# Routing table of an expert layer: the token ids summed from bfloat16 one-hots before the weights, and the first gather issued from the id table inside the routing's block

## The chip, the core and the metric

One core of a Trainium2 chip runs the whole kernel in one launch. Its engines run side by side and meet by semaphores: PE (TensorE) multiplies matrices into PSUM, DVE (VectorE) and ACT (ScalarE) work on elements, POOL (GpSimd) makes constants and issues the indirect DMAs, SP (SyncE) issues the plain ones. The metric is the device time of one execution in microseconds (us): the median of three runs before was 1134.75 (1132.99 to 1135.12).

## The reference, cut to what matters

One decoder layer: 1024 prompt tokens and 64 sample tokens (8 by 8) of width 1024 pass a mixer (attention and convolution), a residual add, a norm, and then 16 experts of which each token uses two.

```
h = rmsnorm(y + mix @ w_out)                       # 1088 rows
g_idx = argmax(h @ w_group + b_group)              # one of 4 groups; g_w its softmax weight
e_val, e_idx = top_k((h @ w_router + b_router)[group g_idx], 2)
e_w = softmax(e_val) * g_w
combine[n, e] = e_w of the two chosen experts, else 0
hid = silu(h @ w_gate[e]) * (h @ w_up[e]) * combine
y = y + sum over e of hid @ w_down[e];  out = rmsnorm(y)
```

## The kernel before, in words

The kernel is a row of blocks: projection, attention, `mix_out` (output projection, residual, norm, routing) and `experts`. A block holds a program for each engine; between two blocks all engines meet in a barrier, which POOL collects and releases. The order inside an engine is as written; nothing is scheduled.

`mix_out` goes over nine tiles of 128 tokens (the last has 64): it stores x1 and the normed h as rows in memory and makes the router's logits. After the last tile comes the routing, most of it a chain on DVE. Each token has two chosen experts (k = 0, 1). The pairs are sorted by expert into blocks of 128 slots, at most MAXB = 32 blocks; `slot_f` is a pair's slot, `block_f` its block and `row_f` its row there. Two tables are wanted, with 128 rows and one column for each block: `slot_ids` (the token of a slot) and `slot_w` (its weight). They come from one-hots: `block_pick` (which block, 32 columns, L1716) is multiplied by the weights (L1718) and by the token numbers plus one (L1720), `row_pick` (which row, 128 columns, L1724, three tiles at a time) turns it, and PE sums `row_pick`^T x `block_pick` over nine tiles, two choices and two halves of the rows: 72 matmuls in float32 (L1834). An empty slot sums to 0 and is given a spare row's number (L1735, L1736). `slot_w` is copied last (L1738). Meanwhile ACT rounds the first expert's up weights (`up_hi`, L1883); each float32 weight tile is kept as a rounded part, `_hi` on ACT, and the remainder, `_rest` on DVE (L1888), and PE multiplies with both.

`experts` goes over the blocks. For each one POOL copies a column of `slot_ids` to `row_id` (L2026) and issues an indirect DMA that gathers 128 rows of h into `landing` (L2029). DVE copies `landing` to `rows` (`fetch`, L2140), PE turns `rows` by transposes (L2212), ACT rounds (`rowsT_hi`) and DVE takes the remainder (`rowsT_lo`, L2145). PE makes gate and up, DVE the product `hid`, PE turns it, ACT and DVE split it (`hidT_hi`, `hidT_lo`), and PE makes y, which ACT and DVE scale by `slot_w` into `y_out`; POOL adds that to x1 in memory. Gathers run ahead: `gather(b)` waits until block b-1's rows were copied out of `landing`. Before the first block DVE makes `up_rest`, then fetches. SP loads the second expert's weights (gate, up, down; 2 MB each) when the first gather has landed, and every later expert's when PE has done with the buffer:

```
sp.wait_ge(gathered, 16)
for which in moe.names:
    moe.load(sp, which, 1, 1)
```

DVE in the first step makes `down_rest` and a half of the next `gate_rest` before `hid`; ACT makes `gate_hi` (a half), silu, `gate_hi` and `up_hi` (a half each) before `hidT_hi`.

Of the kernel before, what the change touches and what calls it, by code (L numbers as in the profile page):

```python
# [24 lines left out]
BF16 = mybir.dt.bfloat16  # L25
# [4 lines left out]
P = 128  # L30
# [1351 lines left out]
def mix_out(nc, io, keep):  # L1382
# [5 lines left out]
    PAIRS = NB // 2  # L1388
    with ExitStack() as stack:  # L1389
# [50 lines left out]
        token_no = p.sb("token_no", [P, TT])  # L1440
# [4 lines left out]

        row_pick = keep["stage"][:, D * KD // 2:D * KD // 2 + 2 * TT * P].rearrange("p (t k x) -> p t k x", t=TT, k=2)
        block_pick = keep["stage"][:, D * KD // 2 + 2 * TT * P:D * KD // 2 + 2 * TT * (P + 2 * MAXB)].rearrange("p (t k v x) -> p t k v x", t=TT, k=2, v=2)
# [77 lines left out]
        def _(pool):  # L1525
# [5 lines left out]
            nc.gpsimd.iota(token_no[:, :], pattern=[[P, TT]], base=1, channel_multiplier=1, **exact).then_inc(consts, 1)  # L1531
            pool.wait_ge(consts, 3)
            nc.gpsimd.memset(token_no[NB * NT:P, QT_N:TT], 0.0).then_inc(consts, 1)
# [15 lines left out]
                                    pattern=[[1, NE], [-1, NE]], channel_multiplier=0).then_inc(consts, 1)  # L1549

        @block.scalar
        def _(act):
# [34 lines left out]
            nc.scalar.activation(e_exp[:, :], e_gap[:, :], ACT.Exp).then_inc(e_exped, 1)  # L1587
            for c in range(2):
                moe.split_hi(act, "up", 0, 0, c)

        @block.vector
        def _(dve):
# [59 lines left out]
            for t in range(TT):  # L1652
# [29 lines left out]
                if t in SELECT_AFTER:  # L1682
# [31 lines left out]

            all_slots = [P, TT, 2, MAXB]
            step(nc.vector.tensor_tensor(block_pick[:, :, :, 0, :], iota_p[:, 0:MAXB].unsqueeze(1).unsqueeze(1).to_broadcast(all_slots),  # L1716
                                         block_f[:, :, :].unsqueeze(3).to_broadcast(all_slots), ALU.is_equal))
            step(nc.vector.tensor_tensor(block_pick[:, :, :, 1, :], block_pick[:, :, :, 0, :],  # L1718
                                         weight[:, :, :].unsqueeze(3).to_broadcast(all_slots), ALU.mult))
            step(nc.vector.tensor_tensor(block_pick[:, :, :, 0, :], block_pick[:, :, :, 0, :],  # L1720
                                         token_no[:, :].unsqueeze(2).unsqueeze(2).to_broadcast(all_slots), ALU.mult))
            for t in range(0, TT, 3):
                part = [P, 3, 2, P]
                nc.vector.tensor_tensor(row_pick[:, t:t + 3, :, :], iota_p[:, :].unsqueeze(1).unsqueeze(1).to_broadcast(part),  # L1724
                                        row_f[:, t:t + 3, :].unsqueeze(3).to_broadcast(part), ALU.is_equal).then_inc(slotted, 1)
            step(nc.vector.memset(ends_f[:, 0:1], 0.0))
# [4 lines left out]
            step(nc.vector.memset(slot_ids[:, MAXB:], 0))  # L1731
            dve.wait_ge(slots_summed, 1)
            numbers = y[0][0][:, 0:MAXB]

            step(nc.vector.tensor_scalar(occupied[:, :], numbers, 0.0, spare_no[:, 0:1], ALU.is_equal, ALU.mult))  # L1735
            step(nc.vector.scalar_tensor_tensor(out=slot_ids[:, 0:MAXB], in0=occupied[:, :], scalar=-1.0, in1=numbers,  # L1736
                                                op0=ALU.add, op1=ALU.add))
            step(nc.vector.tensor_copy(slot_w[:, 1:], y[0][0][:, MAXB:2 * MAXB]))  # L1738

        @block.tensor  # L1740
        def _(pe):
# [150 lines left out]
def experts(nc, io, keep):  # L1892
# [5 lines left out]
    with ExitStack() as stack:  # L1898
# [489 lines left out]
```

## Time and profile before

| | |
|---|---|
| median of three runs | 1134.75 us |
| the profiled execution, its span | 1136.06 us, 1134.3 us |
| PE busy | 1040.3 us (92%) |
| DVE, ACT, POOL busy | 595.7 (53%), 482.1 (43%), 152.5 (13%) us |
| mean granted clock of PE | 0.965 |
| moved by DMA | 207.31 MB, 183 GB/s |

Busy shares are means over stages with different limits. A row of the timeline has the start in us from the span's start, the length in us, the engine, the line of the kernel, the operation, out<-in by names, shapes and the count of merged instructions; in brackets the engine's idle time before and what ended it. `stage` is the buffer that holds `row_pick` and `block_pick`, so their rows carry its name. PEclk is the granted share of PE's full clock: 0.50 is 1.2 GHz, 1.00 is 2.4 GHz.

### The profile page before, as it was taken

What the parts mean: (1) busy time and instruction counts of PE and PEld (TensorE: products, weight loads), DVE (VectorE), ACT (ScalarE), POOL (GpSimd) and SP (SyncE); (2) the same over time, 40 slices, a digit from 0 to 9 for tenths busy, and PEclk for the clock granted to TensorE, in tenths of its full rate; (3) what the DMA queues carried; (4) which work ended last, traced back from release to release, by engine and by line L of the source; (5) the groups of instructions that cost most, each with busy time, mean ns of one, the idle gap of its engine ahead of it and who ended that gap; (6) DMA issues with size and microseconds to landing.
All of it is one profiled execution on the core that took longest, in us unless ns stands there. A gap on an engine that the chain in (4) does not pass through costs nothing. (4 is left out here: it accounts for less than half of the span.)

```text
span 1134.3 us, 16350 instructions
## 1 busy us (share of the span) xinstructions
PE 1040.3 (92%) x5907; PEld 853.1 (75%) x5908; DVE 595.7 (53%) x976; ACT 482.1 (43%) x748; POOL 152.5 (13%) x139
## 2 busy tenths in 40 slices
PE   4999999999899998989999469999999999999990
PEld 3779999999766656648888358888888778888870
DVE  4421351110266664534255755566599967458845
ACT  5431110111466663433333253355468745537544
POOL 0000000000100000000000032122235341323320
PEclk8999999999999999999999679999999999999995
DMA  6416121012540006656332576668799976869766
GB/s 215 130 47 257 56 57 56 13 45 78 137 140 1 1 1 224 264 225 218 125 125 104 184 277 211 184 209 286 252 381 378 370 252 253 296 207 366 245 196 242
DMA packets 95873, 207.31 MB, mean 183 GB/s; under 512 B 12560, under 2 KB 34873, under 8 KB 95787
## 3 DMA queue, kind: packets, MB, share of 16 engines
q1 hardware_dynamic: 88332, 179.89, 44.3%
q0 software_dynamic: 7488, 26.71, 8.8%
q8 instruction: 33, 0.54, 0.2%
q14 instruction: 20, 0.16, 0.0%
HBM read 175.75 MB, written 37.08 MB: 188 GB/s over the span
## 5 line engine op out<-in xcount | busy, mean ns | idle before, releaser
L605 PE MATMUL bank<-xT_hi,w_hi 128*128 128x384 f32 (+1 forms) x432 | 94.6, 327 | 0.0
L605 PE MATMUL bank<-xT_rest,w_hi 128*128 128x384 f32 (+1 forms) x432 | 93.9, 325 | 0.0
L605 PE MATMUL bank<-xT_hi,w_rest 128*128 128x384 f32 (+1 forms) x432 | 93.9, 325 | 0.0
L2048 POOL DMA_INDIRECT x_rows<-y_out,out_id x23 | 57.8, 2512 | 170.5 <-DVE rows L2140 156.4
L2255 PE MATMUL y<-down_hi,hidT_hi 128*128 128x512 f32 x192 | 77.0, 401 | 2.2 <-ACT hidT_hi L2102 2.2
L2220 PE MATMUL gate<-gate_hi,rowsT_hi 128*128 128x512 f32 x192 | 76.7, 399 | 0.7 <-ACT rowsT_hi L2077 0.7
L1888 DVE TENSOR_TENSOR down_rest<-w_down,down_hi 128x2048 fp32r<-128x2048 f32 x32 | 71.9, 2288 | 10.3 <-ACT down_hi L1883 9.4
L2221 PE MATMUL gate<-gate_rest,rowsT_hi 128*128 128x512 f32 x192 | 77.2, 402 | 0.0
L2221 PE MATMUL up<-up_rest,rowsT_hi 128*128 128x512 f32 x192 | 75.7, 394 | 0.0
L1888 DVE TENSOR_TENSOR gate_rest<-w_gate,gate_hi 128x2048 fp32r<-128x2048 f32 x32 | 73.1, 2284 | 4.7 <-ACT gate_hi L1883 4.7
L2220 PE MATMUL up<-up_hi,rowsT_hi 128*128 128x512 f32 x192 | 75.2, 392 | 0.0
L2256 PE MATMUL y<-down_rest,hidT_hi 128*128 128x512 f32 x192 | 75.1, 391 | 0.0
L605 PEld LDWEIGHTS bank<-xT_hi,w_rest 128*128 128x128 f32 x432 | 73.0, 188 | 0.0
L605 PEld LDWEIGHTS bank<-xT_hi,w_hi 128*128 128x128 f32 x432 | 72.7, 188 | 0.2
L605 PEld LDWEIGHTS bank<-xT_rest,w_hi 128*128 128x128 f32 x432 | 72.3, 188 | 0.0
L1888 DVE TENSOR_TENSOR up_rest<-w_up,up_hi 128x2048 fp32r<-128x2048 f32 x32 | 71.8, 2285 | 0.6 <-PEq L1389 0.6
L1883 ACT ACTIVATE up_hi<-w_up 128x2048 fp32r<-128x2048 f32 x32 | 61.5, 1924 | 10.0 <-DMA w_up<-in_w_up 9.9
L1883 ACT ACTIVATE gate_hi<-w_gate 128x2048 fp32r<-128x2048 f32 x32 | 61.3, 1914 | 5.5 <-DMA w_gate<-in_w_gate 5.4
L1883 ACT ACTIVATE down_hi<-w_down 128x2048 fp32r<-128x2048 f32 x32 | 59.7, 1916 | 0.8 <-issue 0.7
L2166 DVE TENSOR_TENSOR hid<-up,silu 128x128 f32<-128x128 f32 (+1 forms) x48 | 18.1, 420 | 71.0 <-PE up L2224 71.0
L998 ACT ACTIVATE logit<-logit,neg_max 128x256 f32<-128x256 f32 (+7 forms) x80 | 52.2, 656 | 6.3 <-DVE neg_max L1082 6.3
L2026 POOL COPY row_id<-slot_ids 128x1 int32 (+1 forms) x26 | 34.3, 1321 | 149.0 <-POOLq L1389 137.3
(310 smaller groups left out, 2083.1 us busy)
## 6 DMA issues: line engine op xcount, KB each, us to landing
w_gate<-in_w_gate SPq DMA_DIRECT2D x16, 2048.0 KB, 12.9
w_up<-in_w_up SPq DMA_DIRECT2D x16, 2048.0 KB, 13.6
w_down<-in_w_down SPq DMA_DIRECT2D x16, 2048.0 KB, 15.4
stage<-in_w_in SPq DMA_DIRECT2D x6, 1536.0 KB, 7.0
k_cache<-in_cache_b_k SPq DMA_DIRECT2D x8, 768.0 KB, 6.7
bias_scratch<-bias_one_row SPq DMA_DIRECT2D x1, 5800.0 KB
mixT<-in_x_prompt SPq DMA_DIRECT2D x8, 512.0 KB, 4.1
x<-in_x_prompt SPq DMA_DIRECT2D x8, 512.0 KB, 4.4
```

The lines of the kernel that those rows point to most:

```text
L605: ins = nc.tensor.matmul(bank[3 * (n % 2) + i][:, 0:m], w_tiles(wt, n // CH + 1)[:, k, cols], xt[:, k, c:c + m], start=(k == 0 and x == 0) ...
L998: nc.scalar.activation(logit[:, u % 4, 0:n], logit[:, u % 4, 0:n], ACT.Exp, bias=neg_max[:, u:u + 1], scale=-1.0, accum_out=denom[:, u:u + ...
L1883: self.nc.scalar.activation(self.hi[which][half][:, k, :], self.raw[which][half][:, k, :], ACT.Copy).then_inc(self.hi_made, 1)
L1888: self.nc.vector.tensor_tensor(self.rest[which][half][:, k, :], self.raw[which][half][:, k, :], self.hi[which][half][:, k, :].bitcast(F32) ...
L2026: nc.gpsimd.tensor_copy(row_id[:, :], slot_ids[:, bass.ds(b, 1)]).then_inc(gather_id, 1)
L2048: nc.gpsimd.indirect_dma_start(out=io["x1"], out_offset=bass.IndirectOffsetOnAxis(ap=out_id[:, :], axis=0), in_=y_out[:, :], in_offset=Non ...
L2166: nc.vector.tensor_tensor(hid[:, cols], up[:, cols], silu[:, cols], ALU.mult).then_inc(hid_ready, 1)
L2220: nc.tensor.matmul(out[:, :], rowsT_hi[:, k, :], hi[:, k, :], start=(k == 0), stop=False)
L2221: nc.tensor.matmul(out[:, :], rowsT_hi[:, k, :], rest[:, k, :], start=False, stop=False)
L2255: nc.tensor.matmul(y[j][:, :], hidT_hi[:, k, :], moe.hi["down"][half][:, k, cols], start=(k == 0), stop=False)
L2256: nc.tensor.matmul(y[j][:, :], hidT_hi[:, k, :], moe.rest["down"][half][:, k, cols], start=False, stop=False)
```

## The change

The sum over slots is split in two. The first sum makes the ids alone. `row_pick_b` (bfloat16) takes the place of `row_pick` in it, and the token numbers enter as whole numbers that bfloat16 holds exactly: ACT makes `row_no` = `block_pick` x (row + 1) for all tiles, and `tile_no` = `block_pick` x 128 t for tiles 1 to 8. PE adds both kinds: 34 matmuls over whole 128 rows. Pairs that don't exist get row -1. Then `slot_ids` is written, and only then DVE multiplies `block_pick` by the weights, writes `ends`, and waits for the second sum: 72 float32 matmuls as before with 32 columns in place of 64, for which ACT converts `row_pick_b` to float32 `row_pick`, before `up_hi`.

POOL issues the first gather at the end of `mix_out`, with a column of `slot_ids` as its index and without a copy, into `first_rows`, a part of `mixT` (free by then). In `experts` the second gather waits for no fetch; DVE fetches first and makes `up_rest` after `rowsT_lo`; SP waits for `rows_ready`, since `first_rows` lies where the second expert's weights go.

On DVE, from the rows of the slots to the second fetch, before (the stage's names stand for `block_pick` and `row_pick`):

```order
L1712 SCALAR_TENSOR_TENSOR row_f<-block_f,slot_f 128x18 [waits dve_step3]
L1716 TENSOR_TENSOR stage<-iota_p,block_f 128x18x32 [waits dve_step3]
L1718 TENSOR_TENSOR stage<-stage,weight 128x18x32 [waits dve_step3]
L1720 TENSOR_TENSOR stage<-stage,token_no 128x18x32 [waits dve_step3]
L1724 TENSOR_TENSOR stage<-iota_p,row_f 128x768 [waits dve_step3]
...
L1735 TENSOR_SCALAR occupied<-y,spare_no 128x32 [waits slots_summed,dve_step3]
L1736 SCALAR_TENSOR_TENSOR slot_ids<-occupied,y 128x32 [waits dve_step3]
L1738 COPY slot_w<-y 128x32 [waits dve_step3]
...
L1888 TENSOR_TENSOR up_rest<-w_up,up_hi 128x2048 [waits weights_hi] x2
L2140 COPY rows<-landing 128x1024 [waits gathered]
L2145 TENSOR_TENSOR rowsT_lo<-turn,rowsT_hi 128x512 [waits rowsT_hi_made] x2
```

and of the changed kernel:

```order
L1733 SCALAR_TENSOR_TENSOR row_f<-block_f,slot_f 128x18 [waits dve_step3]
L1737 MEMSET row_f 64x2 [waits dve_step3]
L1739 TENSOR_TENSOR stage<-iota_p,block_f 128x576 [waits dve_step3]
L1743 TENSOR_TENSOR row_pick_b<-iota_p,row_f 128x768 x3
L1748 TENSOR_SCALAR occupied<-y,spare_no 128x32 [waits slots_summed]
L1749 SCALAR_TENSOR_TENSOR slot_ids<-occupied,y 128x32 [waits dve_step3]
L1753 TENSOR_TENSOR stage<-stage,weight 128x576 [waits gapped,e_exped]
...
L1762 COPY slot_w<-y 128x32 [waits slots_summed,dve_step3]
...
L2170 COPY rows<-mixT 128x1024 [waits gathered]
L2175 TENSOR_TENSOR rowsT_lo<-turn,rowsT_hi 128x512 [waits rowsT_hi_made] x2
L1919 TENSOR_TENSOR up_rest<-w_up,up_hi 128x2048 [waits weights_hi] x2
L2170 COPY rows<-landing 128x1024 [waits gathered,turned5]
```

The product with the weights went behind the ids, the one with the token numbers left DVE, and `up_rest` went behind the first fetch. On POOL, from the routing's last constant to the second gather, before:

```order
L1548 AFFINE_SELECT ahead<-ahead_blocks 128x256 [waits consts3]
L1389 UNCONDITIONAL_BRANCH
L2020 UNCONDITIONAL_BRANCH [waits barrier_Pool_Activation_PE_DVE_SP_gather]
L2026 COPY row_id<-slot_ids 128x1
L2029 DMA landing<-h_rows,row_id 128x1024 [waits gather_id]
L2026 COPY row_id<-slot_ids 128x1 [waits rows_ready]
L2029 DMA landing<-h_rows,row_id 128x1024 [waits gather_id]
```

and of the changed kernel:

```order
L1552 AFFINE_SELECT ahead<-ahead_blocks 128x256 [waits consts3]
L1561 DMA mixT<-h_rows,slot_ids 128x1024 [waits spare_stored,slotted,h_stored1,mix_rest_made,h_stored0]
L1390 UNCONDITIONAL_BRANCH
L2051 UNCONDITIONAL_BRANCH [waits barrier_Pool_Activation_PE_DVE_SP_gather]
L2057 COPY row_id<-slot_ids 128x1
L2060 DMA landing<-h_rows,row_id 128x1024 [waits gather_id]
```

The first gather stands ahead of the barrier, and its copy is gone. On ACT, between the last exponential and the end of the block, the changed kernel has (before, the two `up_hi` followed at once):

```order
L1600 ACTIVATE e_exp<-e_gap 128x9 [waits gapped]
L1603 ACTIVATE row_no<-stage,row_one 128x576 [waits consts3,gapped]
L1605 ACTIVATE tile_no<-stage 128x64 x8
L1608 ACTIVATE stage<-row_pick_b 128x768 [waits slotted] x3
L1914 ACTIVATE up_hi<-w_up 128x2048 [waits up_loaded0]
L1914 ACTIVATE up_hi<-w_up 128x2048
```

Twelve instructions came in ahead of `up_hi`. The diff, cut to its core:

```diff
...
@@ mix_out, POOL
-            nc.gpsimd.iota(token_no[:, :], pattern=[[P, TT]], base=1, channel_multiplier=1, **exact).then_inc(consts, 1)
+            nc.gpsimd.iota(row_one[:, :], pattern=[[0, 1]], base=1, channel_multiplier=1, **exact).then_inc(consts, 1)
...
+            pool.wait_ge(mix_rest_made, TT)
+            pool.wait_ge(h_stored[0], 16 * 5)
+            pool.wait_ge(h_stored[1], 16 * 4)
+            pool.wait_ge(spare_stored, 32)
+            pool.wait_ge(slotted, TT // 3 + 1)
+            nc.gpsimd.sem_inc(consts, 1)
+            nc.gpsimd.indirect_dma_start(out=first_rows, out_offset=None, in_=io["h"],
+                                         in_offset=bass.IndirectOffsetOnAxis(ap=slot_ids[:, 0:1], axis=0)).then_inc(gathered, 16)
@@ mix_out, ACT, behind e_exp
+            act.wait_ge(gapped, 2)
+            act.wait_ge(consts, 4)
+            nc.scalar.activation(row_no[:, :, :, :], block_pick[:, :, :, :], ACT.Copy, scale=row_one[:, :]).then_inc(e_exped, 1)
+            for t in range(1, TT):
+                nc.scalar.activation(tile_no[:, t - 1, :, :], block_pick[:, t, :, :], ACT.Copy, scale=float(P * t)).then_inc(e_exped, 1)
+            for j in range(TT // 3):
+                act.wait_ge(slotted, j + 1)
+                nc.scalar.activation(row_pick[:, 3 * j:3 * j + 3, :, :], row_pick_b[:, 3 * j:3 * j + 3, :, :], ACT.Copy).then_inc(e_exped, 1)
             for c in range(2):
                 moe.split_hi(act, "up", 0, 0, c)
...
@@ mix_out, PE
             for t in range(TT):
-                if t % 3 == 0:
-                    pe.wait_ge(slotted, t // 3 + 1)
+                pe.wait_ge(slotted, t // 3 + 1)
+                pe.wait_ge(e_exped, 2 + t)
+                for k in range(2):
+                    nc.tensor.matmul(y[0][0][:, 0:MAXB], row_pick_b[:, t, k, :], row_no[:, t, k, :], start=(t == 0 and k == 0), stop=False)
+                    if t:
+                        ins = nc.tensor.matmul(y[0][0][:, 0:MAXB], row_pick_b[:, t, k, :], tile_no[:, t - 1, k, :], start=False, stop=(t == TT - 1 and k == 1))
+            ins.then_inc(slots_summed, 1)
+            pe.wait_ge(slotted, TT // 3 + 2)
+            pe.wait_ge(e_exped, 1 + TT + TT // 3)
+            for t in range(TT):
                 for k in range(2):
                     for rows in (slice(0, P // 2), slice(P // 2, P)):
-                        ins = nc.tensor.matmul(y[0][0][rows, 0:2 * MAXB], row_pick[:, t, k, rows],
-                                               block_pick[:, t, k, :, :].rearrange("p v x -> p (v x)"),
+                        ins = nc.tensor.matmul(y[0][1][rows, 0:MAXB], row_pick[:, t, k, rows], block_pick[:, t, k, :],
                                                start=(t == 0 and k == 0), stop=(t == TT - 1 and k == 1))
             ins.then_inc(slots_summed, 1)
@@ experts, SP, POOL and DVE
-            sp.wait_ge(gathered, 16)
+            sp.wait_ge(rows_ready, 1)
...
-                if b is not FIRST:
+                if type(b) is not int or b > 1:
                     pool.wait_ge(rows_ready, b)
...
-            gather(FIRST)
             gather(1)
...
-                nc.vector.tensor_copy(rows[:, :], landing[:, :]).then_inc(rows_ready, 1)
+                nc.vector.tensor_copy(rows[:, :], first_rows if b is FIRST else landing[:, :]).then_inc(rows_ready, 1)
...
-            for c in range(2):
-                moe.split_rest(dve, "up", 0, 0, c)
             fetch(FIRST)
             rows_lo(FIRST, 0)
             rows_lo(FIRST, 1)
+            for c in range(2):
+                moe.split_rest(dve, "up", 0, 0, c)
             fetch(1)
...
@@ program
+        keep["first_rows"] = keep["mixT"][:, 0, 0:D]
```

## Rows read from the trace of the kernel before

**Rows 1.** PE, 676 to 1095 us: who it waited for, total us, times, longest.
```profile
PE y L2255 <- ACT hidT_hi L2102: 2.2, 2, 1.2
PE hturn L2245 <- DVE hid L2166: 1.5, 1, 1.5
```

**Rows 2.** Timeline, ACT and DVE at the second expert's weights (columns as above).
```profile
669.36 1.92 ACT L1883 ACTIVATE gate_hi<-w_gate 128x2048 fp32r<-128x2048 f32 x1 [2.23 <-DMA w_gate<-in_w_gate]
...
675.96 1.91 ACT L1883 ACTIVATE up_hi<-w_up 128x2048 fp32r<-128x2048 f32 x1 [0.96 <-DMA w_up<-in_w_up]
...
677.28 0.75 DVE L2166 TENSOR_TENSOR hid<-up,silu 128x128 f32<-128x128 f32 x2
...
677.98 0.28 ACT L2102 ACTIVATE hidT_hi<-hturn 128x128 fp32r<-128x128 f32 x1
```

**Rows 3.** The same timeline, SP's issues of the second expert's weights.
```profile
659.31 0.38 SPq L1874 DMA_DIRECT2D w_gate<-in_w_gate  x1
...
659.74 0.57 SPq L1874 DMA_DIRECT2D w_up<-in_w_up  x1
```

**Rows 4.** The same timeline, DVE at the end of the routing.
```profile
641.68 0.18 DVE L1712 SCALAR_TENSOR_TENSOR row_f<-block_f,slot_f 128x18 f32<-128x18 f32 x1
...
641.89 0.76 DVE L1716 TENSOR_TENSOR stage<-iota_p,block_f 128x576 f32<-128x576 f32 x1
...
644.27 2.69 DVE L1724 TENSOR_TENSOR stage<-iota_p,row_f 128x768 f32<-128x768 f32 x3
...
649.41 0.25 DVE L1735 TENSOR_SCALAR occupied<-y,spare_no 128x32 f32<-128x32 f32 x1 [1.69 <-PE y L1834]
...
649.70 0.19 DVE L1736 SCALAR_TENSOR_TENSOR slot_ids<-occupied,y 128x32 int32<-128x32 f32 x1
...
649.92 0.19 DVE L1738 COPY slot_w<-y 128x32 f32<-128x32 f32 x1
```

**Rows 5.** The same timeline, PE: the count's first pass, the sum over slots.
```profile
636.95 0.39 PE L1824 MATMUL count<-picks,ones 128*128 128x16 bf16 x9 [4.75 <-DVE picks L1688]
...
645.28 4.01 PE L1834 MATMUL y<-stage 128*64 128x64 f32 x72 [7.32 <-DVE stage L1724]
```

**Rows 6.** ACT by shape, 560 to 680 us (busy, mean ns); one timeline row.
```profile
L1557 ACT ACTIVATE mix_hi<-mixT 128x1024 fp32r<-128x1024 f32 x3 | 3.1, 1046 | 0.0
...
L1585 ACT ACTIVATE g_exp<-g_shift 128x36 f32<-128x36 f32 x1 | 0.2, 233 | 1.0 <-DVE g_shift L1630 1.0
...
641.39 3.71 ACT L1883 ACTIVATE up_hi<-w_up 128x2048 fp32r<-128x2048 f32 x2 [5.36 <-DMA w_up<-in_w_up]
```

**Rows 7.** The timeline, POOL: the first two gathers.
```profile
650.72 2.29 POOL L2026 COPY row_id<-slot_ids 128x1 int32<-128x1 int32 x1 [137.32 <-POOLq L1389]
...
653.95 2.23 POOL L2029 DMA_INDIRECT landing<-h_rows,row_id  x1 [0.94 <-POOL row_id L2026]
...
660.08 0.18 POOL L2026 COPY row_id<-slot_ids 128x1 int32<-128x1 int32 x1 [3.90 <-DVE rows L2140]
...
661.06 0.96 POOL L2029 DMA_INDIRECT landing<-h_rows,row_id  x1 [0.80 <-POOL row_id L2026]
```

**Rows 8.** The timeline, DVE at the start of the experts.
```profile
650.67 4.49 DVE L1888 TENSOR_TENSOR up_rest<-w_up,up_hi 128x2048 fp32r<-128x2048 f32 x2 [0.56 <-PEq L1389]
...
659.32 0.69 DVE L2140 COPY rows<-landing 128x1024 f32<-128x1024 f32 x1 [4.16 <-DMA landing<-h_rows,row_id]
...
662.70 0.69 DVE L2145 TENSOR_TENSOR rowsT_lo<-turn,rowsT_hi 128x512 fp32r<-128x512 f32 x1 [0.16 <-ACT rowsT_hi L2077]
...
669.08 0.69 DVE L2140 COPY rows<-landing 128x1024 f32<-128x1024 f32 x1 [5.69 <-DMA landing<-h_rows,row_id]
```

**Rows 9.** Gathers into landing, from issue to landing.
```profile
DMA to landing us min/median/max: 5.1/8.7/10.0
```

**Rows 10.** Two stretches: busy us of each engine, PEclk, DMA share, GB/s.
```profile
653.00:666.00 13.00, 5.25 (x16) 4.17 (x17) 4.24 (x4) 3.78 (x4) 3.38 (x4) 0.50 0.53 175
...
667.00:680.00 13.00, 11.53 (x57) 9.31 (x56) 9.08 (x10) 9.17 (x10) 4.57 (x3) 1.00 1.03 395
```

More of the change, by code:

```diff
@@ L1388, in mix_out @@
     PAIRS = NB // 2
+    gathered, first_rows = keep["gathered"], keep["first_rows"]
     with ExitStack() as stack:
@@ L1439, in mix_out @@
         weight = p.sb("weight", [P, TT, 2])
-        token_no = p.sb("token_no", [P, TT])
+        row_one = p.sb("row_one", [P, 1])
         spare_no = p.sb("spare_no", [P, 1])
@@ L1446, in mix_out @@
         row_pick = keep["stage"][:, D * KD // 2:D * KD // 2 + 2 * TT * P].rearrange("p (t k x) -> p t k x", t=TT, k=2)
-        block_pick = keep["stage"][:, D * KD // 2 + 2 * TT * P:D * KD // 2 + 2 * TT * (P + 2 * MAXB)].rearrange("p (t k v x) -> p t k v x", t=TT, k=2, v=2)
+        block_pick = keep["stage"][:, D * KD // 2 + 2 * TT * P:D * KD // 2 + 2 * TT * (P + MAXB)].rearrange("p (t k x) -> p t k x", t=TT, k=2)
+        row_pick_b, row_no = keep["row_pick_b"], keep["row_no"]
+        tile_no = p.sb("tile_no", [P, TT - 1, 2, MAXB], BF16)
         zeros = p.sb("zeros", [P, 128])
@@ L1713, in _ @@
                                                 op0=ALU.mult, op1=ALU.add))
+            step(nc.vector.memset(row_f[NB * NT:P, QT_N, :], -1.0))
             all_slots = [P, TT, 2, MAXB]
[L1716 to L1721, printed above, removed]
+            nc.vector.tensor_tensor(block_pick[:, :, :, :], iota_p[:, 0:MAXB].unsqueeze(1).unsqueeze(1).to_broadcast(all_slots),
+                                    block_f[:, :, :].unsqueeze(3).to_broadcast(all_slots), ALU.is_equal).then_inc(gapped, 1)
             for t in range(0, TT, 3):
                 part = [P, 3, 2, P]
-                nc.vector.tensor_tensor(row_pick[:, t:t + 3, :, :], iota_p[:, :].unsqueeze(1).unsqueeze(1).to_broadcast(part),
+                nc.vector.tensor_tensor(row_pick_b[:, t:t + 3, :, :], iota_p[:, :].unsqueeze(1).unsqueeze(1).to_broadcast(part),
                                         row_f[:, t:t + 3, :].unsqueeze(3).to_broadcast(part), ALU.is_equal).then_inc(slotted, 1)
+            dve.wait_ge(slots_summed, 1)
+            numbers = y[0][0][:, 0:MAXB]
+            step(nc.vector.tensor_scalar(occupied[:, :], numbers, 0.0, spare_no[:, 0:1], ALU.is_equal, ALU.mult))
+            nc.vector.scalar_tensor_tensor(out=slot_ids[:, 0:MAXB], in0=occupied[:, :], scalar=-1.0, in1=numbers,
+                                           op0=ALU.add, op1=ALU.add).then_inc(slotted, 1)
+            dve.wait_ge(e_exped, 1 + TT)
+            dve.wait_ge(gapped, 2)
+            nc.vector.tensor_tensor(block_pick[:, :, :, :], block_pick[:, :, :, :],
+                                    weight[:, :, :].unsqueeze(3).to_broadcast(all_slots), ALU.mult).then_inc(slotted, 1)
+            step(nc.vector.memset(slot_ids[:, MAXB:], 0))
             step(nc.vector.memset(ends_f[:, 0:1], 0.0))
@@ L1730, in _ @@
             step(nc.vector.tensor_copy(ends[:, :], ends_f[:, :]))
[L1731 to L1738, printed above, removed]
+            dve.wait_ge(slots_summed, 2)
+            step(nc.vector.tensor_copy(slot_w[:, 1:], y[0][1][:, 0:MAXB]))
         @block.tensor
@@ L1920, in experts @@
         rows_ready = p.sem("rows_ready")
-        gathered = p.sem("gathered")
+        gathered, first_rows = keep["gathered"], keep["first_rows"]
         gather_id = p.sem("gather_id")
@@ L2329, in program @@
             keep["silu"] = q.sb("silu", [P, FF])
+        with ExitStack() as later:
+            q = Pools(nc, later)
+            q.sb("first_rows_place", [P, D])
+            keep["row_pick_b"] = q.sb("row_pick_b", [P, TT, 2, P], BF16)
+            keep["row_no"] = q.sb("row_no", [P, TT, 2, MAXB], BF16)
         keep["mixT"] = p.sb("mixT", [P, 8, TOK])
@@ L2351, in program @@
                 attend(nc, io, keep)
+        keep["gathered"] = p.sem("gathered")
+        keep["first_rows"] = keep["mixT"][:, 0, 0:D]
         moe.place(p, 0)
```

4 lines of the change are left out of this document (2 added, 2 removed).

## The prediction

> **What bounds the kernel now.** I began with the page: PE is busy for 92% of the span, and its row of slices shows one clear hole, in the slice where attention's output has been projected and the experts have not begun. The waits of PE from 676 us to the last expert say the same from the other side: in over 400 us it waits 3.7 us in all, and all of that beside the first expert's hidden rows [rows 1]. From there on PE sets the time, and every weight load is released by PE's progress, so whatever the first expert's hidden rows gain reaches the end.
>
> So the timeline around those rows came next [rows 2]. ACT splits three weight tiles of the second expert in a row; the first waited for w_gate and began at 669.36, the last waited for w_up and began at 675.96. It ended at 677.87, and hidT_hi, queued behind it on ACT, began at 677.98, just when PE's turned rows were there. Two chains meet here within 0.1 us: the hidden rows (DVE's hid at 677.28) and the second expert's weights. The weights start when SP issues them, at 659.31, 659.74 and after [rows 3]: w_gate needs 10.05 us, w_up 16.2 us, with the DMA rings at 395 GB/s [rows 10]. SP waits for the first gather. So both chains hang on one thing: when the first block's rows of h have landed.
>
> Then backward from there. DVE's table work ends with row_pick, the three comparisons from 644.27 to 646.96; PE sums 72 pieces until 649.29; slot_ids is written by 649.89, slot_w by 650.11 [rows 4, 5]. The experts' block opens 0.56 us later: up_rest begins at 650.67 [rows 8], and POOL copies the ids (2.29 us) and issues the gather at 653.95 (2.23 us) [rows 7]. The rows land at 659.3, 9.4 us after the ids were written. The second gather's same two steps took 0.18 and 0.96 us. The first ones ran beside up_rest, 650.67 to 655.16; the copy ended at 653.01, with the first half of up_rest (2.29 us a half), and the issue 1.0 us after the second half.
>
> The Trainium skill ("SBUF — State Buffer", Who interferes with whom) states that a DVE instruction with two SBUF inputs blocks a GpSimd instruction that reads SBUF; the copy agrees with that (2.29 against 0.18 us). The same section infers that it doesn't hold back descriptor generation; the issue's 2.23 against 0.96 us speaks against this part. By the page the second gather could not be held by up_rest, which would strike rival 2 below; by the row it could.
>
> **The change, part by part.**
>
> Ids. DVE's two products over block_pick leave the path; they are 576 wide like the comparison at 641.89, which took 0.76. A memset of row_f comes in; I charge it a whole step, the 0.21 from row_f's start to the next. block_pick then runs 642.10 to 642.86, and three row_pick_b comparisons (2.69 together, same width) end at 645.56 instead of 646.96. Their output type changes; I leave the price.
>
> Beside them ACT makes row_no and eight tile_no. ACT's price is read from 1.046 us at 1024 columns and 0.233 at 36 [rows 6], that is 0.20 + 0.82 per 1000 columns: 0.68 for row_no (576), 0.26 for each tile_no (64). Two instructions in a row overlap by 0.1 (3.71 for two up_hi [rows 6], 1.91 for one [rows 2]), so the eight cost 1.2 to 2.1, and ACT is through between 644.8 and 645.7: level with DVE.
>
> PE's id sum is 34 matmuls with bfloat16 weights; the nearest row is the nine of the count, 0.39 us together, 0.043 each [rows 5]. When the last row_pick_b comes, 12 are left: 0.5 us. The other bound is the old pace, 4.01/72 = 0.056, with all 34 after the last comparison: 1.9 us. I take 0.5 and 0.1 for the wait: the sum ends at 646.2 (at worst 647.6). The ids follow 0.60 after, as from 649.29 to 649.89: 646.8, at worst 648.2, instead of 649.89.
>
> First gather. POOL needs no copy; it waited 0.80 to 0.94 before each issue [rows 7], which I keep: issue at 647.7. It takes 0.96 alone or 2.23 beside DVE. The product with the weights, moved behind the ids, runs 646.9 to 647.6 and is over by then. In the profile the rows landed 3.1 us after the issuing ended, so 651.8; the shortest from issue to landing is 5.1 us [rows 9], which gives 652.8, or 654.2 with the late ids. No other transfer runs then.
>
> The block's end. This is now what comes last. ACT converts three row_pick pieces (768 columns, 0.84 each), which begins when its small pieces are done: the last ends between 646.4 and 648.2. Then up_hi, 3.71, until 650.1 to 651.9; before it was done by 645.1, so work that cost nothing now reaches the path. PE's second sum waits for the converted pieces and for the weighted block_pick (647.7); 72 matmuls with the same stationary width and half the columns cost 2.0 to 4.0, so they end between 649.8 and 652.2, and slot_w stands 0.3 later. DVE's five small steps on ends lie under this. Block entry is 0.56 after the last: 651.0 to 653.1; I take 652.6, near the upper end, where the measured 4.01 stands.
>
> First rows. DVE's fetch, now first in the experts' block, starts at the later of entry and landing, 652.6 (bounds 651.5 and 654.2), instead of 659.32; with 0.69 for the copy rows_ready comes at 653.3. SP now waits for rows_ready, not for the landing; so its loads start at 653.3 instead of 659.31: **6.0 us earlier** (4.4 to 7.1). That is the term which counts. The rows themselves come 6.7 earlier (660.01).
>
> What is late next. up_rest lost its cover: it used to lie under the gather's landing and now stands between rows_lo and the second fetch. rows_lo ended 3.38 us after the rows were copied (663.39 after 660.01 [rows 8]), so 656.7; up_rest's 4.49 gives 661.2. The up product begins when gate is through, 7.4 us after gate's start at 656.0 with the clock at half (0.50 until 666 [rows 10]) and earlier at full clock by less than 2 us: up_rest is in time or barely late. The second gather waits no longer for rows_ready. POOL's copy may stand behind DVE's fetch (to 653.5), the issue follows at 654.3 and ends at 655.3; at 7.0 us from there, as with the weights in flight before (662.02 to 669.05), it lands at 662.3, and the second fetch ends at 663.0. From there to hid it was 7.51 us (669.77 to 677.28): 670.5, a gain of 6.8. w_up lands 6.0 earlier, at 669.9; up_hi ends at 671.9 and hidT_hi follows. So the weights' 6.0 stays the smaller gain and PE gets 6.0. A faster PE clock in this stretch gives nothing: PE would wait for the same two.
>
> Sum: the profiled execution took 1136.06 us, 1.8 more than its span of 1134.3 and 1.3 above the median of the runs, 1134.75. 1136.06 - 6.0 = 1130.1 for that execution, and against the median 1134.75 - 6.0 = **1128.75, I say 1128.8 us**.
>
> **The rivals.**
> 1. The block's end holds more than I gave it. For it: ACT gets 12 instructions more on the path, and waits between engines of 0.1 us are hardly in my sum. If the chain of conversions, second sum and slot_w comes 1 to 3 us later (entry 654.3 to 656), the gain is 2.3 to 4.4: 1130.4 to 1132.5. Against it: each price has a near row.
> 2. The second gather is held by up_rest, as the first was. Condition: its issue isn't through at 656.7; I have it through at 655.3, 1.4 us of margin. Behind one half of up_rest it would end at 656.7 + 2.29 + 0.96 = 659.9, land at 666.9, and hid would come at 675.2: 2.1 gained, 1132.7. Behind both, the issue ends at 662.1, hid comes at 677.2: nothing gained, 1134.7.
> 3. Slower: the same holding behind both halves, and a landing of 10.0 us from the issue, the longest in the trace [rows 9], because the weights are then in full flight. Issue at 661.2, landing 671.2, hid 679.4: 2.1 later than now, 1136.9. It decides from the point where landing plus 0.69 plus 7.51 passes 677.28, that is a landing after 669.1. Against it: both must come together.
> 4. More: the weights are not the limit (they land sooner in a freer stretch) and entry is early, at 651.5. Then hid's gain of 6.8 grows to 7.9: 1126.9. Against it: 395 GB/s is steady in the trace.
> 5. The first gather doesn't run ahead, since POOL's queue reaches it late or the block's end waits for its landing. The five semaphores it waits for are all met before the ids, and a landing at 651.8 before the block's end adds at most 0.6: this only joins rival 1.
>
> **How the numbers follow.** Forecast (4.4 to 7.1 gained) 0.60; rival 1 with 5, 0.15; rival 2, 0.11; rival 3, 0.04; rival 4, 0.10. About 0.2% of this kernel, 2.3 us, can be told from no change. Faster: forecast, rivals 1 and 4, less a hundredth, 0.84. Same: rival 2 (2.1 and 0 gained) and that hundredth, less some for noise to either side, 0.11. Slower: rival 3 and a hundredth of rival 2, 0.05. The range holds the forecast, rival 4 nearly whole and two thirds of rival 1: 1126.7 to 1131.7.
>
> **What would show it.** Right: slot_ids written near 646.8; the first DMA_INDIRECT near 647.7 with a length near 1.0; DVE's first fetch at 652.6, ended waiting by the block's opening and not by the landing; SP's w_gate at 653.3; ACT's second up_hi in the experts' block still waiting for w_up, and hidT_hi 6 us earlier; PE's waits after 670 as few as before. Wrong: the fetch waits for the landing after 653; up_hi in the routing block ends after 653; the second DMA_INDIRECT takes over 2 us; or PE waits for up_rest before the first up product.

## The result and the profile after

The changed kernel took 1125.9 us (median of 4 runs, 1123.21 to 1126.21) beside 1134.37 us for the kernel before (4 runs, 1132.99 to 1135.12): the ratio of the times is 0.9917 [0.9902, 0.9932]. That is 8.5 us by the medians, where 6.0 were forecast, and 0.8 us below the range. Two later pairings gave 0.9921 [0.9902, 0.994] and 0.9936 [0.9914, 0.9957].

The timeline of the changed kernel, from DVE's row_f to the third expert's first weight load (start in us, length in us, engine, line, operation, tiles, and in brackets the idle time before it with what ended it):

```profile
639.67 0.18 DVE L1733 SCALAR_TENSOR_TENSOR row_f<-block_f,slot_f 128x18 f32<-128x18 f32 x1
...
640.68 2.69 DVE L1743 TENSOR_TENSOR row_pick_b<-iota_p,row_f 128x768 bf16<-128x768 f32 x3
...
641.48 1.26 ACT L1605 ACTIVATE tile_no<-stage 128x64 bf16<-128x64 f32 x8
...
643.42 0.21 PE L1857 MATMUL y<-row_no,row_pick_b 128*128 128x32 bf16 x1 [0.27 <-DVE row_pick_b L1743]
...
644.25 0.19 DVE L1749 SCALAR_TENSOR_TENSOR slot_ids<-occupied,y 128x32 int32<-128x32 f32 x1
...
644.85 3.69 ACT L1914 ACTIVATE up_hi<-w_up 128x2048 fp32r<-128x2048 f32 x2
...
645.16 4.05 PE L1866 MATMUL y<-stage 128*64 128x32 f32 x72 [1.23 <-DVE stage L1753]
645.50 1.14 POOL L1561 DMA_INDIRECT mixT<-h_rows,slot_ids  x1 [134.38 <-DVE stage L1753]
649.33 0.19 DVE L1762 COPY slot_w<-y 128x32 f32<-128x32 f32 x1 [3.47 <-PE y L1866]
...
650.31 0.69 DVE L2170 COPY rows<-mixT 128x1024 f32<-128x1024 f32 x1 [0.79 <-PEq L1390]
650.37 0.68 POOL L2057 COPY row_id<-slot_ids 128x1 int32<-128x1 int32 x1 [3.73 <-POOLq L1390]
651.03 0.38 SPq L1905 DMA_DIRECT2D w_gate<-in_w_gate  x1
651.46 0.57 SPq L1905 DMA_DIRECT2D w_up<-in_w_up  x1
651.84 0.97 POOL L2060 DMA_INDIRECT landing<-h_rows,row_id  x1 [0.79 <-POOL row_id L2057]
...
659.95 0.69 DVE L2170 COPY rows<-landing 128x1024 f32<-128x1024 f32 x1 [1.17 <-DMA landing<-h_rows,row_id]
...
667.00 1.91 ACT L1914 ACTIVATE up_hi<-w_up 128x2048 fp32r<-128x2048 f32 x1 [0.47 <-DMA w_up<-in_w_up]
668.15 0.75 DVE L2196 TENSOR_TENSOR hid<-up,silu 128x128 f32<-128x128 f32 x2
...
668.86 0.28 ACT L2132 ACTIVATE hidT_hi<-hturn 128x128 fp32r<-128x128 f32 x1
...
680.90 0.41 SPq L1905 DMA_DIRECT2D w_gate<-in_w_gate  x1
```

The row of the kernel before that answers to the last of these is

```profile
690.02 0.41 SPq L1874 DMA_DIRECT2D w_gate<-in_w_gate  x1
```

Read all of them against [rows 4, 7, 8, 2, 3] as well, and count from row_f in both traces. The ids start 4.58 us after row_f instead of 8.02, the gather's issue 5.83 instead of 12.27, DVE's copy of the first rows 10.64 instead of 17.64, SP's first load 11.36 instead of 17.63, DVE's copy of the second rows 20.28 instead of 27.40, hid 28.48 instead of 35.60. The third expert's first load, which PE's progress releases, starts 41.23 after row_f instead of 48.34: 7.1 us gained in this stretch, as much as the copy of the second rows gained. The two profiled spans differ by 10.1. The other 3.0 lie outside: row_f itself stands at 639.67 instead of 641.68 (2.0), and the third load to the end takes 443.3 instead of 444.3 (1.0).

PE's waits from 655 to 1090 us (total us, times, longest) answer to [rows 1]; the pair of chains still meets there, hidT_hi at 668.86 with up_hi from 667.00 just over:

```profile
PE y L2285 <- ACT hidT_hi L2132: 2.1, 2, 1.2
PE hturn L2275 <- DVE hid L2196: 1.0, 1, 1.0
```

Three stretches just before the experts' block opens, and w_up's way from its issue to its split (length, busy us of PE, its weight loads, DVE, ACT and POOL, then PE's granted clock, DMA share and GB/s):

```profile
648.00:649.00 1.00, 1.00 (x24) 1.00 (x22) 0.00 (x0) 0.54 (x1) 0.00 (x0) 0.50 0.92 356
649.00:649.50 0.50, 0.22 (x5) 0.08 (x2) 0.17 (x1) 0.00 (x0) 0.00 (x0) 0.50 0.49 180
649.50:650.00 0.50, 0.00 (x0) 0.00 (x0) 0.02 (x1) 0.00 (x0) 0.00 (x0) 0.50 0.00 0
...
651.46:667.00 15.54, 14.85 (x58) 11.77 (x57) 11.94 (x9) 10.52 (x8) 5.14 (x4) 0.80 0.97 347
```

The last two columns matter: the traffic ends by 649.50, and slot_w, the last of the second sum, is written by 649.52. DVE's copy follows at 650.31, 0.8 us after both, ended waiting by the block's opening. From this trace alone nobody can say which of the two it waited for.

### The profile page after: what moved, and what is told of

Same layout as the page of the kernel before. It is cut to its first block and busy times, and to the rows that moved or that the text cites. A ratio compares the mean times of both kernels' runs of the same rounds, so it can differ in the third digit from the quotient of the medians.

```text
span 1124.2 us, 16421 instructions
## 1 busy us (share of the span) xinstructions
PE 1041.0 (93%) x5941; PEld 854.3 (76%) x5942; DVE 594.3 (53%) x976; ACT 486.3 (43%) x760; POOL 145.5 (13%) x138
## 5 line engine op out<-in xcount | busy, mean ns | idle before, releaser
L2078 POOL DMA_INDIRECT x_rows<-y_out,out_id x23 | 49.2, 2140 | 177.9 <-DVE rows L2170 163.8
L2132 ACT ACTIVATE hidT_hi<-hturn 128x128 fp32r<-128x128 f32 (+1 forms) x48 | 18.2, 383 | 80.0 <-PE hturn L2275 80.0
```

The costliest lines, as they stand in the source:

```text
L2078: nc.gpsimd.indirect_dma_start(out=io["x1"], out_offset=bass.IndirectOffsetOnAxis(ap=out_id[:, :], axis=0), in_=y_out[:, :], in_offset=Non ...
L2132: nc.scalar.activation(hidT_hi[:, k0:k1, :], hturn[c][:, 0:(k1 - k0) * P].rearrange("p (k c) -> p k c", c=P), ACT.Copy).then_inc(hidT_hi_m ...
```

## The experiments

Throughout, "third load" is the third expert's first weight load, counted from row_f; it was 48.34 before and 41.23 in the changed kernel. Where times are compared, the ratio is to the kernel before on the same chip.

**The two kernels again.** No edit; the changed kernel twice more, the kernel before twice more.

> The changed kernel once more, for its time over more rounds and a second profile. In the first pair of profiles the routing's chain stood 2.0 us earlier before any changed instruction (row_f began at 639.67 against 641.68), 7.2 us were gained between row_f and the third expert's first load, and 1.0 us after that. Theory 1: only the 7.2 us come from the change; the rest is stretches of half clock in attention that differ from one execution to the next, so row_f lands anywhere between 639 and 642.5 here, the length from row_f to the third expert's load is again within 0.3 us of 41.2, and over five rounds the gain comes to 7 to 7.6 us (ratio 0.9933 to 0.9938). Theory 2: the new program also runs its unchanged parts faster, by 1 to 2 us: row_f again within 0.3 us of 639.7 and a gain of 8.2 to 9 us (0.9921 to 0.9928).

> The kernel before, timed against itself. Both theories: ratio 1.000 within 0.1%. Theory 1: row_f in its profile moves by up to 2 us from 641.68 while the length from row_f to the third expert's load stays at 48.3 within 0.4 us. Theory 2: row_f stays within 0.3 us of 641.7.

The changed kernel: third load 41.26 and, beside a later experiment, 41.36. The kernel before: 50.44 here (ratio to itself 0.999 [0.9974, 1.0007]) and 47.92 in a further profile. So the changed kernel repeats its stretch within 0.13 us, and the kernel before does not repeat its own within 2.5, where 0.4 was expected. The first expectation is met by half: row_f and the stretch came as its first theory has them, the ratio, 0.9921, as its second; the interval holds both. The mean gain over three profiles each is 48.90 - 41.28 = 7.6. Row_f stands at 641.68, 639.72 and 637.63 before and at 639.67, 640.54 and 639.16 after: no part of the gain is there, so I take the 2.0 between the first two profiles for scatter.

From the profile with 50.44, one wait of PE and two stretches (columns as above):

```profile
PE hturn L2245 <- DVE hid L2166: 2.4, 1, 2.4
```
```profile
674.00:677.00 3.00, 0.83 (x8) 0.83 (x9) 2.73 (x4) 1.95 (x2) 0.00 (x0) 1.00 1.02 408
677.00:680.00 3.00, 3.00 (x11) 2.32 (x10) 2.31 (x5) 2.70 (x4) 0.00 (x0) 0.54 0.31 124
```

PE waited 2.4 us for hid instead of 1.5; behind it the granted clock was 0.54 over 3 us, close to the lower level (1.2 GHz), where [rows 10] have 1.00, and 11 matmuls filled the stretch. This is where the kernel before lost 2 us more in one profile of three. The further profile, with 47.92, was taken to see whether the half clock follows a long wait: there PE waited 1.3 us for hid and the clock stayed at 1.00. But a kernel below waited 2.2 and kept the clock too, so the wait alone does not decide.

The rest of that scatter lies in one place. The second gather landed 7.1, 7.9 and 6.8 us after its issue's end in the three profiles of the kernel before, and DVE's copy of the second rows began 27.40, 27.91 and 26.97 after row_f. Hid followed 8.2 later each time, and so it did in the changed kernel (8.20, 8.21, 8.20). From hid to the third load it was 12.7 to 12.8 in five of the six, and 14.3 in the one with the half clock. So this stretch hangs on the second gather's landing: DVE's queue goes on from that copy through down_rest and a half of gate_rest to hid.

**Order only.** The kernel before, with DVE's up_rest moved behind the first fetch as in the change; ids, sums and gather as before.

```diff
-            for c in range(2):
-                moe.split_rest(dve, "up", 0, 0, c)
             fetch(FIRST)
             rows_lo(FIRST, 0)
             rows_lo(FIRST, 1)
+            for c in range(2):
+                moe.split_rest(dve, "up", 0, 0, c)
```

> The kernel before with one part of the change: DVE makes up_rest after the first fetch and rowsT_lo, not before. Theory A (up_rest held POOL's id copy and the issue behind it): the copy takes 0.2 us instead of 2.29 and the issue 1.0 instead of 2.23, so the rows land 3.3 to 3.5 us sooner after the block's opening (5.2 instead of 8.65), SP's loads go as much earlier and the kernel gains 3 to 3.6 us. Theory B (both are slow because they are the first of their kind in the block): the copy stays near 2.3 and the issue near 2.2, the fetch stays where it is and nothing is gained (0 to 0.5 us).

Measured 1130.33 us, 0.997 [0.9954, 0.9986]; third load 45.25. POOL and DVE in the timeline:

```profile
646.13 0.19 POOL L2026 COPY row_id<-slot_ids 128x1 int32<-128x1 int32 x1 [137.37 <-POOLq L1389]
647.26 1.14 POOL L2029 DMA_INDIRECT landing<-h_rows,row_id  x1 [0.94 <-POOL row_id L2026]
...
651.74 0.69 DVE L2140 COPY rows<-landing 128x1024 f32<-128x1024 f32 x1 [6.21 <-DMA landing<-h_rows,row_id]
```

The copy takes 0.19 instead of 2.29 and the issue 1.14 instead of 2.23 [rows 7]; the rows are fetched 14.68 after row_f instead of 17.64. Nothing else was edited, so up_rest held both. Of the 7.1 us this order alone gives 3.1.

**The change with the old order.** The reverse: up_rest back ahead of the first fetch.

```diff
+            for c in range(2):
+                moe.split_rest(dve, "up", 0, 0, c)
             fetch(FIRST)
             rows_lo(FIRST, 0)
             rows_lo(FIRST, 1)
-            for c in range(2):
-                moe.split_rest(dve, "up", 0, 0, c)
```

> The changed kernel with up_rest put back in front of the first fetch. The rows have landed when the block opens, so the fetch waits for up_rest alone: both theories have it 4.5 us later and SP's loads with it, and the time 4 to 4.6 us above the changed kernel (3.9 to 4.5 us still gained against the kernel before). They differ at the second gather: theory A has POOL's copy near 2.3 us and the issue near 2.2 beside up_rest; theory B has 0.2 to 0.7 and 1.0, since the first gather went before.

Measured 1131.92 us, 0.9972 [0.9956, 0.9989]; third load 46.43.

```profile
647.76 4.49 DVE L1919 TENSOR_TENSOR up_rest<-w_up,up_hi 128x2048 fp32r<-128x2048 f32 x2 [0.79 <-PEq L1390]
647.82 2.28 POOL L2057 COPY row_id<-slot_ids 128x1 int32<-128x1 int32 x1 [3.74 <-POOLq L1390]
650.89 2.20 POOL L2060 DMA_INDIRECT landing<-h_rows,row_id  x1 [0.79 <-POOL row_id L2057]
652.17 0.69 DVE L2170 COPY rows<-mixT 128x1024 f32<-128x1024 f32 x1
...
669.69 1.91 ACT L1914 ACTIVATE up_hi<-w_up 128x2048 fp32r<-128x2048 f32 x1 [1.20 <-DMA w_up<-in_w_up]
```

The lock is back, now on the second gather: 2.28 for its copy and 2.20 for its issue. The rows, which landed long before, are copied 15.06 after row_f instead of 10.64, so SP's loads start at 15.78 and ACT waits 1.20 for w_up. The third load comes 5.2 later than in the changed kernel, where 4 to 4.6 us were expected: hid came 4.3 later, and the rest is the weights, which now decide. The Trainium skill ("SBUF — State Buffer", Who interferes with whom) infers that a DVE instruction of this kind does not hold up the making of an indirect DMA's descriptors. The issue as a whole was held here: it took 2.23 and 2.20 beside up_rest, 1.14 and 0.97 without it. An issue also reads its ids from SBUF, and the rows do not part that reading from the making of the descriptors, so which of the two was held is not shown.

**The change without the early gather.** Split sums and new order stay; the first gather is issued in the experts' block, with its copy of the ids, as before.

```diff
-            pool.wait_ge(slotted, TT // 3 + 1)
-            nc.gpsimd.indirect_dma_start(out=first_rows, ...
...
+            gather(FIRST)
```

> The changed kernel with the first gather put back behind the barrier (copy, then issue, up_rest behind the first fetch as in the change). All counted from row_f's start. If the early issue is what the early ids are for: the block opens at 10.6 as in the changed kernel, the copy takes 0.2, the issue runs 11.7 to 12.7, the fetch comes at 15.8 instead of 10.64, SP's first load at 16.5 instead of 11.36, and the third expert's first load at 46.2 to 46.6 instead of 41.2: 5 us of the gain lost, and worse than the order alone (45.25), since the block now opens 1.65 us later. Rival: the early ids carry most of the gain by themselves; then the third expert's load stays below 44.

Measured 1131.13 us, 0.9979 [0.9965, 0.9992]; third load 46.76.

```profile
646.28 0.19 DVE L1753 COPY slot_w<-y 128x32 f32<-128x32 f32 x1 [3.46 <-PE y L1857]
647.08 0.19 POOL L2048 COPY row_id<-slot_ids 128x1 int32<-128x1 int32 x1 [138.68 <-POOLq L1390]
648.21 1.14 POOL L2051 DMA_INDIRECT landing<-h_rows,row_id  x1 [0.94 <-POOL row_id L2048]
```

Row_f was at 636.62, so slot_w stands at 9.66 and not at 8.27 as with the order alone. The split sums by themselves cost 1.4 us of block, and the third load is 1.5 later than with the order alone. That is the expectation's first reading, with 46.2 to 46.6 expected; the rival, below 44, is out.

**The early gather with the old sums.** Order and early gather; one float32 sum for ids and weights, as before.

```diff
+            pool.wait_ge(slotted, TT // 3 + 1)
+            nc.gpsimd.indirect_dma_start(out=first_rows, ...
...
-                moe.split_rest(dve, "up", 0, 0, c)
             fetch(FIRST)
...
+                moe.split_rest(dve, "up", 0, 0, c)
```

> The kernel before with the gather issued in the routing's block and DVE's new order, but with the old sum (ids and weights in 72 float32 matmuls). Counted from row_f: slot_ids written at 8.2, issue at 9.1 to 10.2, landing and fetch at 13.2 to 13.4, SP's first load at 14.0, the third expert's first load at 43.8 to 44.4 (before 48.3, changed kernel 41.2): the split sums are worth 2.6 to 3.2 us beside the early issue. Rival: the split sums give nothing, because the block's end is held by the weights' sum anyway; then the third expert's load is at 41 to 42.

Measured 1131.38 us, 0.9979 [0.9969, 0.999]; third load 45.57, where 43.8 to 44.4 was expected. Timeline, and two stretches:

```profile
651.10 0.18 DVE L1748 COPY slot_w<-y 128x32 f32<-128x32 f32 x1
652.24 1.14 POOL L1558 DMA_INDIRECT mixT<-h_rows,slot_ids  x1 [137.68 <-issue]
656.79 0.69 DVE L2149 COPY rows<-mixT 128x1024 f32<-128x1024 f32 x1 [5.50 <-PEq L1390]
```
```profile
655.00:656.00 1.00, 0.00 (x0) 0.00 (x0) 0.00 (x0) 0.00 (x0) 0.00 (x0) 0.50 0.85 348
656.00:657.00 1.00, 0.00 (x0) 0.00 (x0) 0.21 (x1) 0.00 (x0) 0.15 (x1) 0.50 0.00 0
```

DVE is done at 651.28, and then PE, DVE and ACT stand idle while the gather's bytes move at 348 GB/s until 656. The copy of the rows at 656.79 was ended by the block's opening, not by a semaphore of its own. So with the issue inside the block, the block stays shut until the rows have landed. This kernel gains nothing over the order alone. Its second gather was issued 1.0 earlier after row_f than with the order alone, but landed 8.2 us after the issue's end instead of 6.9, which used that up; why it took longer is not shown. Its PE waited 2.2 us for hid at a granted clock that stayed at 1.00 afterwards, which is the exception named above.

**No second sum.** To part the landing from the second sum, which end together in the changed kernel, the second sum and its conversions are left out: slot_w then holds token numbers and not the weights.

```diff
-                nc.scalar.activation(row_pick[:, 3 * j:3 * j + 3, :, :], ...
-            dve.wait_ge(slots_summed, 2)
-            step(nc.vector.tensor_copy(slot_w[:, 1:], y[0][1][:, 0:MAXB]))
+            step(nc.vector.tensor_copy(slot_w[:, 1:], y[0][0][:, 0:MAXB]))
-                        ins = nc.tensor.matmul(y[0][1][rows, 0:MAXB], ...
```

> The changed kernel without the second sum, its three conversions on ACT and the wait for it; slot_w gets the token numbers instead of the weights, so the experts' rows are scaled by wrong numbers. It asks what opens the experts' block. Theory 1 (POOL reaches the barrier only when its gather has landed): up_hi ends 2.3 us sooner and DVE is done by 6.5 from row_f, and the block still opens 0.7 us after the landing, at 10.2 to 10.6; the fetch moves by less than 0.4 us from 10.64. Theory 2 (the second sum and slot_w open it, as I predicted): the block opens when ACT is done, near 7.6, and the fetch then waits for the landing itself and comes at 9.8 to 10.0.

One execution, 1127.23 us; third load 41.54. Timeline, and three stretches:

```profile
642.94 3.69 ACT L1902 ACTIVATE up_hi<-w_up 128x2048 fp32r<-128x2048 f32 x2
645.80 1.14 POOL L1561 DMA_INDIRECT mixT<-h_rows,slot_ids  x1 [134.07 <-DVE stage L1750]
646.21 0.19 DVE L1758 COPY slot_w<-y 128x32 f32<-128x32 f32 x1
650.34 0.69 DVE L2158 COPY rows<-mixT 128x1024 f32<-128x1024 f32 x1 [3.94 <-PEq L1390]
650.39 0.68 POOL L2045 COPY row_id<-slot_ids 128x1 int32<-128x1 int32 x1 [3.46 <-POOLq L1390]
```
```profile
649.00:650.00 1.00, 0.00 (x0) 0.00 (x0) 0.00 (x0) 0.00 (x0) 0.00 (x0) 0.50 0.42 168
650.00:651.00 1.00, 0.00 (x0) 0.00 (x0) 0.66 (x1) 0.00 (x0) 0.60 (x1) 0.50 0.00 0
...
651.49:667.64 16.15, 14.98 (x60) 11.77 (x58) 12.61 (x9) 10.53 (x9) 5.15 (x4) 0.83 0.98 350
```

From 646.94 on, when POOL's issue ends, no engine has work; PE, DVE and ACT have none from 646.63, 3.7 us before the opening. POOL's copy of the second ids waits for no rows, and it too begins only at 650.39: the block itself was shut. The copy of the rows comes 10.37 after row_f instead of 10.64. Taking the whole second sum away moves the opening by 0.3 us: the landing sets it, and the second sum is hidden under it to within that. The third load is 0.3 later all the same, though hid came at 28.16, 0.3 earlier: w_up took 16.15 us here, and the weights decided (13.4 us from hid to the third load instead of 12.7). That bears out the forecast's two chains, and shows how little lies between them.

**Both gathers in the routing block.** The second gather is issued there too, straight behind the first, into the second expert's down buffer, whose weights are then loaded only when DVE has copied the rows out.

```diff
+            nc.gpsimd.indirect_dma_start(out=keep["second_rows"], out_offset=None, in_=io["h"],
+                  in_offset=bass.IndirectOffsetOnAxis(ap=slot_ids[:, 1:2], axis=0))...
...
-            gather(1)
```

> The changed kernel with the second gather issued in the routing's block too, right behind the first and into another place, and the second expert's down weights loaded when DVE has fetched it. Theory 1 (the second fetch and the weights, not PE, hold the first expert's hidden rows by the 0.7 to 1.0 us that PE waited): the second fetch comes at 19.1 from row_f instead of 20.3, w_up lands up to 1.3 us sooner, PE no longer waits for hid, and the third expert's first load comes at 40.2 to 40.5 instead of 41.2; 0.7 to 1 us gained on the changed kernel. Theory 2 (PE's own work is the limit there): the load stays at 41.2. If the second issue delays the first rows or the barrier, the first fetch moves from 10.64 to 11 or 12 and the load to 41.5 to 42.

Measured 1129.12 us, 0.9955 [0.9937, 0.9973]; third load 43.72, 2.5 later than in the changed kernel.

```profile
646.75 1.14 POOL L1560 DMA_INDIRECT mixT<-h_rows,slot_ids  x1 [133.83 <-DVE stage L1755]
648.18 0.95 POOL L1563 DMA_INDIRECT w_down<-h_rows,slot_ids  x1 [0.30 <-issue]
650.58 0.19 DVE L1764 COPY slot_w<-y 128x32 f32<-128x32 f32 x1 [3.46 <-PE y L1868]
654.31 0.69 DVE L2178 COPY rows<-mixT 128x1024 f32<-128x1024 f32 x1 [3.54 <-PEq L1390]
```

The block stays shut 3.5 us beyond slot_w: it now waits for the second landing. The copy of the rows comes at 13.39 instead of 10.64, where 12 was the worst expected, and the whole kernel pays for it, although PE no longer waits for hid. Together with the two kernels above, this shows what the opening follows: the landing of what was issued in the block.

**Another order in the first block.** The changed kernel, with DVE's second fetch moved behind the first step's split of down (down_rest), and ACT's split of the second expert's up behind its rows_hi.

```diff
-            fetch(1)
...
+                if b is FIRST:
+                    fetch(1)
...
-                    moe.split_hi(act, "up", *following, 0)
+                if following and b is FIRST:
+                    moe.split_hi(act, "up", *following, 0)
```

> The changed kernel with two orders changed in the first expert's step: DVE fetches the second block's rows behind down_rest instead of ahead of it, and ACT makes the second expert's up_hi behind hidT_hi and rowsT_hi. Counted from row_f. Theory 1 (in the changed kernel the second gather's landing at 20.3 and ACT's queue hold the first hidden rows, and PE waits 0.7 to 1.0 us for them): down_rest starts near 19.5 instead of 21.9, hid comes at 27.3 to 27.8 instead of 28.5, as soon as PE has up, and the third expert's first load comes at 40.2 to 40.6 instead of 41.25. Theory 2 (the later fetch and up_hi come back as waits in the second expert): PE waits for rowsT or up_rest there and the load stays at 41.2 or later.

> The changed kernel beside e9 on the same chip. Stretch from row_f to the third expert's first load 41.2 to 41.3 as in its two profiles; a ratio of 0.991 to 0.994 against the kernel before.

Measured 1123.0 us (1121.1 to 1126.93), 0.9905 [0.9882, 0.9927]; the changed kernel on the same chip 1127.24, 0.9936 [0.9914, 0.9957].

```profile
658.56 2.29 DVE L1919 TENSOR_TENSOR down_rest<-w_down,down_hi 128x2048 fp32r<-128x2048 f32 x1
660.76 0.69 DVE L2173 COPY rows<-landing 128x1024 f32<-128x1024 f32 x1
664.62 0.76 DVE L2201 TENSOR_TENSOR hid<-up,silu 128x128 f32<-128x128 f32 x2 [0.97 <-PE up L2258]
```

Row_f was at 637.29: hid comes at 27.33 instead of 28.48, the wait of PE for it is gone from the list of its waits (the two for hidT_hi, 2.0 us, remain), and the third load stands at 40.10, 1.2 earlier. DVE finds the rows landed and does not stand idle for them. Which of the two orders gave the 1.2 was not tried. By the stretch this version beats both kernels; by the times the two intervals overlap, so that 1.2 us is not resolved there.

## Why the prediction was wrong

What held, in its own order. *Ids:* forecast at 646.8, which is 5.1 after row_f (measured, with its length, 4.77); half of the 0.35 is DVE's comparisons, which ended 3.70 after row_f and not 3.88, and the rest is small steps behind them. PE's last id matmuls waited for DVE (row 643.42), not for ACT, whose eight tile_no took 1.26 us. *First gather:* forecast 6.0 after row_f and 0.96 long; measured 5.83 and 1.14. *First rows:* forecast 10.92; measured 10.64. *SP's loads:* forecast 11.62, 6.0 us earlier; measured 11.36, 6.27 earlier. *Late next:* hid forecast at 28.8, a gain of 6.8; measured 28.48, a gain of 7.1. Up_rest was in time, and the second gather was not held (0.97). Rivals 2 and 3 did not occur, but the hold they feared is real: with the old order it fell on that gather. Three slips in the sums did not move the forecast: by its own prices eight tile_no cost at least 1.3, not 1.2; the block's entry has a lower bound of 650.7, not 651.0; and rival 1's entries are 1.7 to 3.4 later, not 1 to 3, which gives 2.6 to 4.3 gained. And 395 GB/s is the rate of [rows 10]; over w_up's way it was 350.

What failed:

1. **"So the weights' 6.0 stays the smaller gain and PE gets 6.0."** PE got 7.1, which is what the second gather and hid gained. The failed step is the size of w_up's way from SP's issue to ACT's split: taken at 16.2 us from one trace, it took 15.54 here (the last of the windows above), 15.27 in the repeat and 14.78 in the changed kernel's third profile. In these last two hidT_hi stood waiting for PE's turned rows, 0.3 and 0.8 us, and not for the weights: hid's chain decided. The way scatters: 16.15 without the second sum, where the stretch has the same transfers, and 15.99 in another profile of the kernel before. In all of these the rate was 344 to 352 GB/s, so a shorter way is not a faster one; fewer bytes of others went by before w_up's last (15.54 x 347 = 5.39 MB, 16.15 x 350 = 5.65 MB). Whose bytes they were is not shown; w_down's are the likeliest, since the way took 13.49 with two early gathers, where w_down was issued 8.0 us behind w_up instead of 0.6. Rival 4 had named this case with 0.10, but its further gain was to come from an early opening, at 651.5, which is not how it came.

2. **"PE's second sum ... I take 652.6, near the upper end, where the measured 4.01 stands."** The second sum did measure 4.05, and the opening came 0.3 before the forecast. But the sum is not what opens the block: without it the opening is 0.3 earlier, with a later landing it is 2.8 later (13.39). Rival 5 had the mechanism, that the block's end waits for the landing, and gave it at most 0.6. The number was right by luck: in this kernel both end together.

3. **The range**, 1126.7 to 1131.7, was made of the bounds of terms and took the base as one number. The stretch before measured 48.34, 50.44 and 47.92 in three profiles; the first was not its mean, 48.90. What moved it was the second gather's landing and, once, the half clock. With 7.6 for the mean gain, 1134.75 - 7.6 = 1127.2, inside the range. The timed gain is 7.3 to 9.4 by the three ratios; 7.6 lies just outside the first pairing's interval (7.7 to 11.1 us) and inside the other two. The up to 1.8 us left are not clear of the noise, and I could not place them: row_f and the tail (443.0 to 444.8 us in all profiles) show no order by kernel.

How the 7.1 is made, by one profile each: the order alone 3.1; early gather on top of it with the old sums -0.3; split sums on top of it without the early gather -1.5; both together 4.0. All of it passes through the second gather: DVE's copy of its rows begins 27.40 after row_f before, 24.28 with the order alone, 24.63, 25.81 and 20.28 with the others, and the third load stands 20.9 to 21.0 behind it each time. The ids' early end is worth something only when a gather uses it, and the early gather is worth something only when the ids come while the block has other work to do. I had priced the parts as a sum along one path, which holds for the whole change and for none of its parts alone.

## What to carry to other kernels

An indirect DMA that is issued early inside a block is not free of that block: if the block's end waits for its landing, as here, issue it so early that the landing falls under the block's last work, and put no second one behind it. Before crediting a gain to a moved transfer, try the plain reordering alone: here two lines moved on DVE gave 3.1 of 7.1 us, because the instruction beside the gather's issue was holding it. And a range needs the scatter of the kernel before in the stretch that changes, which one profile doesn't show.

## What was not expected of the hardware

The lock of POOL by up_rest covers the issue of an indirect DMA as well as the copy: 2.20 to 2.23 us beside it, 0.95 to 1.14 without. In the kernels here that issue an indirect DMA in the routing's block, the next block opens about 0.8 us after the traffic stops (649.50 to 650.31 here, 656.0 to 656.79 with the old sums), with the compute engines idle meanwhile for as long as it takes (3.7 us without the second sum, 3.5 with two gathers). That it is POOL's own queue which waits there is an inference; the trace shows only the opening. The second sum took 4.05 us for 72 float32 matmuls with 32 columns, against 4.01 with 64 columns [rows 5]: half the columns saved nothing.
